# Which wait holds back the eighth and ninth load of expert weights: the first gather of token rows, or the stores of these rows

## What is computed

```python
n2 = _rmsnorm(h, norm2_g[i]) * (1.0 + sc2) + sh2
moe = _hier_moe(n2.reshape(bsz * seq, d), w_grp[i], b_grp[i], w_er[i], b_er[i], w1[i], w3[i], w2[i])
h = h + g2 * moe.reshape(bsz, seq, d)

# in _hier_moe: each token picks one of 8 groups, and 2 of its 8 experts
    xb = xt[buf_tok].reshape(n_blocks, MOE_BLOCK, d)
    def expert_block(args):
        xblk, e = args
        hdn = jax.nn.silu(xblk @ w1[e]) * (xblk @ w3[e])
        return hdn @ w2[e]
```

## Time and profile before

| | |
|---|---|
| median of 3 runs | 2421.54 us |
| the profiled execution | 2422.83 us, span 2421.0 us |
| TensorE matmul busy | 2247.0 us (93%) |
| VectorE busy | 1051.0 us (43%) |
| ScalarE busy | 718.7 us (30%) |
| GpSimd busy | 784.1 us (32%) |
| DMA | 598.75 MB, mean 247 GB/s |
| loads of expert weights | 60 of 4 MB, 71 of 2 MB, 4 of 0.5 MB, 37 us from issue to landing (median, the whole loads) |

### The profile page before, as it was taken

One profiled execution on the slowest core, in us unless ns is written; L12 is line 12 of the kernel. 1 busy time (PEld: TensorE's weight loads), 2 busy tenths in 40 slices (PEclk: granted clock), 3 DMA queues, 4 the chain that ended last, 5 costly groups with the idle time before them and its releaser, 6 DMA issues.

```text
span 2421.0 us, 26169 instructions
## 1 busy us (share of the span) xinstructions
PE 2247.0 (93%) x10596; PEld 1407.1 (58%) x10596; DVE 1051.0 (43%) x1730; ACT 718.7 (30%) x1163; POOL 784.1 (32%) x491
## 2 busy tenths in 40 slices
PE   8999999999999999999999999888888888888887
PEld 6676578888887787777777873222222222222222
DVE  6666644543456999746775233111111111111112
ACT  5435643222233333557674221000000000000001
POOL 3335655554553443433326521111111111111100
PEclk9999999999999999999999999989999899899999
DMA  4222243634645243243445269999999999999997
GB/s 162 99 101 67 97 140 106 208 123 162 203 122 139 70 105 105 80 167 112 139 157 205 104 251 410 425 426 426 427 428 427 427 428 428 428 428 428 429 425 279
DMA packets 167033, 598.75 MB, mean 247 GB/s; under 512 B 17138, under 2 KB 95986, under 8 KB 148736
## 3 DMA queue, kind: packets, MB, share of 16 engines
q1 hardware_dynamic: 147616, 564.38, 59.8%
q10 hardware_dynamic: 8704, 24.22, 2.6%
q0 software_dynamic: 10592, 8.46, 1.1%
HBM read 593.19 MB, written 28.97 MB: 257 GB/s over the span
## 4 chain that ended last, share of the span: by engine, by line
PE 57%; DMA 30%; DVE 10%; ACT 1%; issue 1%; POOL 1%; ACTq 0%; DVEq 0%; SPq 0%; POOLq 0%
DMA expert<-in_wx 29%; PE ps L866 12%; PE ps L867 11%; PE ps L868 11%; PE ps L1429 8%; DVE ps L2491 5%; PE ps L1452 1%; PE ps L1110 1%; PE ps L1086 1%; PE ps L1020 1%; PE ps L965 1%; PE ps L1022 1%; PE ps L1021 1%; PE ps L1077 1%; PE ps L1247 1%
## 5 line engine op out<-in xcount | busy, mean ns | idle before, releaser
L2938 POOL TENSOR_TENSOR ring_r<-ring,ring_r 128x1024 fp32r<-128x1024 f32 (+2 forms) x215 | 513.3, 2394 | 648.4 <-ACT ring_r L1555 648.3
L1429 PE MATMUL ps<-expert,arena 128*64 128x512 f32 x1024 | 509.1, 655 | 132.4 <-DMA expert<-in_wx 131.1
L866 PE MATMUL ps<-r,ring_r 128*128 128x512 f32 x1512 | 605.2, 400 | 2.4 <-DVE arena L2479 1.2
L868 PE MATMUL ps<-r,ring_r 128*128 128x512 f32 x1512 | 590.0, 390 | 0.0
L867 PE MATMUL ps<-r,ring_r 128*128 128x512 f32 x1512 | 589.6, 390 | 0.0
L1431 PE MATMUL ps<-expert,arena 128*64 128x512 f32 x1024 | 509.1, 655 | 0.0
L1566 ACT ACTIVATE arena<-ps 128x512 f32<-128x512 f32 (+4 forms) x200 | 150.6, 761 | 1043.5 <-PE ps L1431 846.0
L1429 PEld LDWEIGHTS ps<-expert,arena 128*64 128x64 f32 x1024 | 147.8, 150 | 464.6 <-issue 305.3
L1555 ACT ACTIVATE ring_r<-ring 128x1024 fp32r<-128x1024 f32 x220 | 222.7, 1015 | 349.0 <-PE ps L868 193.4
L866 PEld LDWEIGHTS ps<-r,ring_r 128*128 128x128 f32 x1512 | 283.0, 187 | 73.7 <-issue 11.2
L3043 POOL DMA_INDIRECT y_d<-arena,cbm x64 | 63.8, 997 | 800.0 <-DVE arena L2883 525.8
(11 more groups left out here) (371 smaller groups left out, 2197.4 us busy)
## 6 DMA issues: line engine op xcount, KB each, us to landing
expert<-in_wx SPq DMA_DIRECT2D x60, 4096.0 KB, 37.2
expert<-in_wx SPq DMA_DIRECT2D x71, 2048.0 KB, 37.1
ring<-in_w_ada SPq DMA_DIRECT2D x12, 2048.0 KB, 8.0
ring<-in_ffn_w_in SPq DMA_DIRECT2D x22, 1024.0 KB, 7.6
ring<-in_w_in SPq DMA_DIRECT2D x40, 512.0 KB, 6.1
ring<-in_w_in SPq DMA_DIRECT2D x8, 2048.0 KB, 9.1
ring<-in_fox_w_in SPq DMA_DIRECT2D x7, 2048.0 KB, 8.5
arena<-acs_d SPq DMA_DIRECT2D x16, 512.0 KB, 3.6
```

The lines of the kernel that those rows point to most:

```text
L866: e.matmul(out, wh[:, k, :], X.hi[:, k0 + k, :], start=first and k == 0, stop=False)
L868: m = e.matmul(out, wl[:, k, :], X.hi[:, k0 + k, :], start=False, stop=last and k == nk - 1)
L1429: e.matmul(u.ap[0:64], x, cols(w1, 8)[:, k, :], start=k == 0, stop=k == 7)
L2938: e.tensor_tensor(GL[t], grans[t][1], GH[t].bitcast(F32), ALU.subtract).then_inc(sem["gr_lo"], 1)
```

## The change

One wait of SyncE's queue is replaced. Before the eighth load of expert weights (and so the ninth, which is issued behind it), SyncE waits for the four stores of the token rows to have landed, and no longer for the first gather of them.

```diff
                     if i == 7:
 
-                        w.wait_ge(sem["xg0"], 16)
+                        w.wait_ge(sem["n2d0"], 32)
+                        w.wait_ge(sem["n2d1"], 32)
```

## The result

The changed kernel takes 2429.47 us (median of 6 runs, 2428.66 to 2431.38); the kernel before takes 2421.41 us in the same comparison (6 runs, 2420.73 to 2423.44). The ratio is 1.0034, with a 95% interval of 1.0024 to 1.0044: 8.1 us slower, between 5.8 and 10.7. 2428.9 was forecast.

A forecast was written before the change was run, and what follows sets the result against it. The stream of expert weights was taken to set the end. Gather's delay 7.4 us plus clock 1.5 minus 1.5 gives +7.4 us on the median 2421.54, so 2428.9 us, range 2424.5 to 2432.5.

The forecast's parts named there:

- The stream sets the end: Last 970 us, one stream of expert weights at DMA share 1.00: moving the whole stream moves the end equally.
- The two loads go out 4.1 us earlier: SyncE's queue: the eighth load goes out at about 1447.2 instead of 1451.32, the ninth right behind it.
- The gather lands 7.4 us later: First gather of token rows on GpSimd, beside 4 MB of loads: lands at 1458.7, 7.4 us later, ends 5.2 and 8.4.
- the nearest row, the third gather: A gather in the kernel before, started 1.9 us after the same loads; packets end 10.3 us after its start, time taken over.
- The clock costs 1.5 us, at most 2.4: TensorE after 8.6 us idle, at a granted clock of about half: 1.5 us lost, ends of 0 and 2.4.
- Less 1.5 us that the stream had in hand: At the tenth load: shift is the gather's delay plus clock loss, minus 1.5 us.
- Sum: Whole kernel: gather's delay plus clock loss minus 1.5 gives +7.4 us, none of it given back later.
- The first, no slower: Queue between 1448 and 1452: the gather is not hurt, its few packets get through; 2420.0 us, chance 0.09.
- Its limit of 1.5 us: Most that can be won, since the tenth load hangs on expert 0 and first shows at 1461.6.
- The second, a smaller loss: First gather's packets begin on time, delay 5.2 us, clock nothing to 1.5 us: +3.7 to +5.2, 2425.2 to 2426.7; chance 0.14.
- the third: The change does nothing: the stores' semaphores reach SyncE no sooner than the gather lands; 2421.5 us, chance 0.05.

The follow-up runs named there:

- no_first_gather: The changed kernel without the first gather; experts 0 and 1 work on rows already in that buffer, results left out; 2418.71 us, 0.9982 of the kernel before.
- quarter_early: The kernel before, but the first 0.5 MB of the eighth load go out once the token-row stores have landed, the rest behind the gather; 2423.30 us, ratio 1.0009.

## Why the prediction was right, step by step

- *The stream sets the end.* Right. The hole filled without another opening (no_first_gather) gives 2.9 us by the medians; in the profiled executions every delay of the tenth load arrives at the end but for about 2 us.
- *The two loads go out 4.1 us earlier.* Right: 0.93 us before the gather's start instead of 3.08 behind it, 4.0 us. They drain later than I put it, though: their last packet stands in the slice from 1459 to 1460, at least 12.3 us behind the gather's start, and I had 11.2. I mixed one gather into them; two ran beside them, which is the likely reason.
- *The gather lands 7.4 us later.* Right, 10.47 - 3.07 = 7.4; the nearest row, the third gather, was the right one to take. That it fits to 0.1 us is luck: in the other kernels with both loads whole and early the gather landed after 10.50 to 11.22 us. What I read into that row was only half right: I saw its packets taking turns with the loads', and took the late start as given. The runs show a hold and the turns as two terms of their own, and the hold does not depend on the size of the packets.
- *The clock costs 1.5 us, at most 2.4.* Mis-sized: 2.9 us. I took 1.6 and 2.4 us from the stretches behind two waits of 2.30 and 4.19 us and reduced them. Here the clock stayed at half for 7.6 us behind the restart, where it was under 5 us there. The longer wait does not explain it, since quarter_early lost 2.7 us behind 2.23 us of idleness; what sets the length of the slow stretch stays open.
- *Less 1.5 us that the stream had in hand.* Nearly: 1.8 us in the profiled executions, 10.29 - 8.06 = 2.2 with the medians' shift, whose interval (5.8 to 10.7) is much wider than the difference.
- *Sum.* 7.4 + 2.9 - 1.8 = 8.5 by the profile, 8.1 by the medians, 7.4 forecast. The two errors have opposite signs, and the clock's is the larger one; the measured shift lies 0.7 us above the forecast, well inside its range.
- *The rivals.* The first, no slower, falls with the gather's 10.47 us. Its limit of 1.5 us was worked out with expert 0 no earlier than before; in no_first_gather, where nothing waits for a gather and the tenth load leaves 1.1 us sooner, 2.9 us were won by the medians, which fits that limit. The second, a smaller loss, falls with the same 10.47 us and the half clock; the third with the issue at 1445.72.

## What to carry to other kernels

A hole in a transfer that bounds the kernel may be the room that a small, awaited transfer needs: before filling it, look at what lands in it and what the stream itself needs from that landing. Here the tenth load hung on the first gather through expert 0, so 4 us given to two loads nobody waited for cost 10 us at the load that everything waited for. Price a small transfer beside a large one by a row where it really ran beside one, and add what the idle engine's clock costs after the wait; here a wait of 2.2 us cost nearly as much clock as one of 8.7 us.

## What the runs showed of the hardware that was not expected

- A gather of 128 rows shows its first packet 1.8 us behind its start when alone. Beside 2 MB or more of loads it takes 4.4 to 4.9 us, with packets of 16 KB and of 2 KB alike. What holds it is not shown by these runs; that it takes less with less in the queues is (first packet after 1.9 us with 0.5 MB and 2.9 us with 1 MB ahead, 4.5 with 2 MB and 4.6 with 4 MB).
- A semaphore that GpSimd raises behind an indirect transfer in its program was up before that instruction is shown to start: SyncE acted on it 0.2 us ahead of the first gather's start, and 1.1 us ahead of the second's. In these two kernels it did not put the other queue's transfer behind the gather.
- Behind 2.23 us without a matmul (quarter_early) stood a stretch at half the clock, behind 1.2 us (the kernel before) none, and that stretch cost twice as much as the gather's own delay (2.7 and 1.2 us). Behind 8.69 us it cost 2.9.
